# Combining after the experts: old rows, norm and parameters loaded into freed weight slots, next weights loaded at the last expert product

## The reference

```
for i in range(DEPTH):                                    # DEPTH = 2
    mix = s5_and_attention(h) if i == 0 else rglru(h)
    h = layer_norm(ALPHA * h + mix, ln1_g, ln1_b)
    h = layer_norm(ALPHA * h + hier_moe(h), ln2_g, ln2_b)
return h[:, N_META:]
# hier_moe: group by argmax, the two best of its 8 experts per token,
#   y[t] = sum over the 2 experts of gate * (silu(x w_gate) * (x w_up)) w_down
# 32 experts, w_gate and w_up 1024x512, w_down 512x1024
# rglru: z = h @ w_in (1024x2560), a convolution over 4 rows, two gates per block of 128
#   channels (10 blocks), a linear recurrence, gelu(gate) * recurrence @ w_out
```

## Time and profile before

| | |
|---|---|
| Time before | 2360.14 us median of 3 runs (2353.16 to 2363.47) |
| The profiled execution | 2359.76 us, its span 2357.8 us |
| PE busy | 2188.0 us (93%) |
| DVE busy | 766.4 us (33%) |
| ACT, POOL busy | 486.0 us (21%), 308.5 us (13%) |
| Granted TensorE clock, mean | 0.96 of full speed |
| DMA | 529.81 MB, mean 225 GB/s |
| First combining | about 1179 to 1251 us |
| Second combining | about 2298 us to the end |

### The profile page before, as it was taken

The page is one execution under the profiler, slowest core; times in us unless marked ns, Lnnn a source line. Parts: engine busy times, 40 slices in busy tenths (PEclk is TensorE's granted clock), DMA queues, the critical chain, the costliest instruction groups (busy, mean ns, idle before and its releaser), DMA issues. The chain is left out here.

```text
span 2357.8 us, 33523 instructions
## 1 busy us (share of the span) xinstructions
PE 2188.0 (93%) x13475; PEld 1240.7 (53%) x13475; DVE 766.4 (33%) x1608; ACT 486.0 (21%) x904; POOL 308.5 (13%) x263
## 2 busy tenths in 40 slices
PE   7999999999689999999968999999967999999994
PEld 5787656655454555455434555555544455545541
DVE  7652236652611111111173444442261111111116
ACT  2222236611001001000023444431100100100001
POOL 7253000011011111111030000001101111111102
PEclk9999999999789999999988999999978999999998
DMA  4110002112399999899885111111239999989987
GB/s 159 38 37 1 21 1 72 32 40 70 141 401 418 420 419 418 343 398 410 368 298 165 40 32 29 40 39 37 71 135 395 414 421 418 420 350 393 413 367 306
DMA packets 148199, 529.81 MB, mean 225 GB/s; under 512 B 43874, under 2 KB 66946, under 8 KB 131664
## 3 DMA queue, kind: packets, MB, share of 16 engines
q1 hardware_dynamic: 134608, 493.84, 53.2%
q0 software_dynamic: 13312, 33.84, 3.7%
q10 hardware_dynamic: 128, 0.02, 0.0%
HBM read 499.99 MB, written 39.98 MB: 229 GB/s over the span
## 5 line engine op out<-in xcount | busy, mean ns | idle before, releaser
L1884 PE MATMUL l_main_pgu<-l_w_ring,l_ex_xT 128*64 128x256 f32 (+1 forms) x4992 | 473.5, 385 | 11.8 <-DMA l_w_ring<-in_l_moe_w_gate 8.5
L1884 PEld LDWEIGHTS l_main_pgu<-l_w_ring,l_ex_xT 128*64 128x64 f32 (+1 forms) x4992 | 285.6, 129 | 188.9 <-issue 41.5
L1930 PE MATMUL l_main_py<-l_w_ring,l_ex_hT 128*64 128x512 f32 (+1 forms) x1248 | 231.9, 595 | 1.9 <-DVE l_ex_hT L2002 1.9
L1881 PE MATMUL l_main_pgu<-l_w_ring,l_ex_xT 128*128 128x512 f32 x384 | 170.1, 597 | 1.7 <-DMA l_w_ring<-in_l_moe_w_gate 1.6
L1998 DVE TENSOR_TENSOR l_ex_hid<-l_ex_sil,l_main_pgu 128x256 f32<-128x256 f32 (+1 forms) x76 | 35.2, 463 | 376.0 <-PE l_main_pgu L1884 278.8
L2343 PE MATMUL lru_pr<-h2T,lru_wz 128*128 128x352 f32 (+1 forms) x480 | 144.4, 462 | 10.3 <-ACTq L2398 10.3
L2002 DVE COPY l_ex_hT<-l_main_ph 128x256 f32<-128x256 f32 (+1 forms) x76 | 35.4, 466 | 363.7 <-PE l_main_ph L1905 363.7
L2361 PE MATMUL lru_pg<-h2T,lru_wz 128*128 128x512 f32 x320 | 148.7, 592 | 0.0
L1930 PEld LDWEIGHTS l_main_py<-l_w_ring,l_ex_hT 128*64 128x64 f32 (+1 forms) x1248 | 69.2, 127 | 132.1 <-issue 124.8
L1976 ACT ACTIVATE l_ex_sil<-l_main_pgu 128x256 f32<-128x256 f32 (+1 forms) x76 | 31.7, 417 | 464.9 <-PE l_main_pgu L1884 372.5
L2343 PEld LDWEIGHTS lru_pr<-h2T,lru_wz 128*128 128x128 f32 x480 | 92.6, 193 | 63.1 <-ACTq L2398 10.7
(11 more groups left out here) (462 smaller groups left out, 2719.8 us busy)
## 6 DMA issues: line engine op xcount, KB each, us to landing
l_w_ring<-in_l_moe_w_gate SPq DMA_DIRECT2D x64, 2048.0 KB, 25.7
l_w_ring<-in_l_moe_w_up SPq DMA_DIRECT2D x64, 2048.0 KB, 27.2
l_w_ring<-in_l_moe_w_down SPq DMA_DIRECT2D x64, 2048.0 KB, 32.2
l_y<-expert_rows SPq DMA_DIRECT2D x32, 512.0 KB, 7.7
h_rows<-H SPq DMA_DIRECT2D x24, 512.0 KB, 5.2
lru_wz<-in_l_w_in SPq DMA_DIRECT2D x20, 512.0 KB, 5.1
w_in<-in_l_w_in SPq DMA_DIRECT2D x4, 2048.0 KB, 9.0
H<-h_rows SPq DMA_DIRECT2D x16, 512.0 KB, 9.8
```

Source lines behind the costliest of these rows:

```text
L1881: last = pe.matmul(out[:], x[:, k, :], w[0][:, k, :], start=k == 0, stop=k == KD - 1)
L1884: last = pe.matmul(out[HALF * h + o:HALF * h + o + m, 0:256], x[:, k, it.at + o:it.at + o + m], w[n][:, k, 256 * h:256 * h + 256], start=k ...
L1930: last = pe.matmul(py[b][HALF * h + o:HALF * h + o + m, :], hT[:, c % 2, HALF * (c // 2) + o:HALF * (c // 2) + o + m], ws[n][:, c, 512 * h ...
```

## The change

Slots 6 to 8 of the ring take the old rows of all tiles (`ROW_UNITS`), slot 9 takes gain, bias and the RG-LRU's parameters (`NORM_UNIT`). SP issues these loads in the experts' part, ahead of the overflow blocks: old rows after the last products that read units 86 to 88, the others after the last that reads unit 89. A new semaphore `ring_free`, set by PE behind the overflow blocks, releases the RG-LRU's weights of blocks 0 and 1, which SP issues before it waits for `rows_done`. Only y rows are loaded per tile, in six buffers in place of four, and they are released when PE has summed them. Tile 0 goes through `y_sum` as the others; DVE takes the old rows from the new tile `h1_rows` and writes to `K.H`. In layer 0 nothing waits for the stores at the phase's end; the RG-LRU's projection does, 10 blocks later. The parameters are loaded as 80 rows of 128 channels, turned by PE in the next phase (a transpose that `prm_turned` announces) and copied by DVE; w_out is loaded behind that.

```diff
+ROW_UNITS, NORM_UNIT = (6, 7, 8), 9
...
                 if u >= UNITS:
-                    r_was, kind_was = W.units[u - UNITS]
...
+                    unit_used(u - UNITS)
                 load_unit(sp, E, u, kind, e, E.loaded[u % UNITS])
+            for unit in range(3 * NE):
+                if unit + UNITS >= 3 * NE and unit % UNITS in ROW_UNITS:
+                    unit_used(unit)
+            combine.load_rows(sp)
+            for unit in range(3 * NE):
+                if unit + UNITS >= 3 * NE and unit % UNITS == NORM_UNIT:
+                    unit_used(unit)
+            combine.load_norm(sp)
             sp.wait_ge(ya_ready, acts[N])
...
             over.tensor(pe)
+            pe.sem_inc(ring_free, 1)
             combine.tensor(pe)
...
-    BUFFERS = 4
+    BUFFERS = 6
...
+    def load_rows(self, sp):
+        for i in range(self.first, NT):
+            t0, m = TILES[i]
+            sp.dma_start(self.rows[0:m, i, :], self.K.h1_dram[t0:t0 + m, :]).then_inc(self.rows_loaded, 16)
+
+    def load_norm(self, sp):
+        self.norm.load(sp, self.A[self.L + "_ln2_g"], self.A[self.L + "_ln2_b"])
+        if not self.last_layer:
+            self.K.lru.load_parameters(sp, self.free)
...
             if j >= B:
-                sp.wait_ge(self.z_done, 2 * (j - B + 1))
+                sp.wait_ge(self.y_summed, 2 * (j - B + 1))
...
-            sp.dma_start(K.H[0:m, self.first + j, :], K.h1_dram[t0:t0 + m, :]).then_inc(self.loaded[j % B], 16)
...
+        if not self.last_layer:
+            sp.wait_ge(self.ring_free, 1)
+            K.lru.load_weights(sp, 0, 0)
+            K.lru.load_weights(sp, 1, 1)
+        sp.wait_ge(self.rows_done, 1)
+        for j in range(B):
+            load(j)
+        for j in range(self.n):
...
+        if self.last_layer:
+            sp.wait_ge(self.stored, 16 * self.n)
...
+        dve.wait_ge(self.rows_loaded, 16 * self.n)
+        for j in range(self.n):
...
+            for h in range(2):
+                c = slice(512 * h, 512 * h + 512)
+                dve.wait_ge(self.y_summed, 2 * j + h + 1)
+                dve.scalar_tensor_tensor(out=self.K.H[0:m, i, c], in0=self.rows[0:m, i, c], scalar=ALPHA, in1=self.ps[j % 2][h][0:m, :],
+                                         op0=ALU.mult, op1=ALU.add).then_inc(self.z_done, 1)
...
         for j in range(n + 3):
-            if 0 < j < n:
+            if j < n:
                 y_sum(j)
...
+    def load_parameters(self, sp, at):
+        self.prm_rows = at("lru_prm_rows", [P])
+        rows = lambda r, m: self.prm_rows[r * NB:(r + m) * NB, :]
+        sp.dma_start(rows(0, 4), self.A["l1_conv_w"].rearrange("j (n p) -> (j n) p", p=P)).then_inc(self.loaded, 16)
+        for j, nm in enumerate(("l1_conv_b", "l1_lru_b_a", "l1_lru_b_x", "l1_lru_lambda")):
+            sp.dma_start(rows(4 + j, 1), self.A[nm].rearrange("(n p) -> n p", p=P)).then_inc(self.loaded, 16)
...
         def _(sp):
+            sp.wait_ge(prm_turned, 1)
             load_w_out(sp, K, 1)
...
+            sp.wait_ge(*K.h2_stored)
             project.sync(sp)
...
         @block.tensor
         def _(pe):
+            pe.wait_ge(R.loaded, 5 * 16)
+            pe.transpose(pa[0][:, 0:8 * NB], R.prm_rows[0:8 * NB, :], K.ident[0:8 * NB, 0:8 * NB]).then_inc(prm_turned, 1)
...
-            dve.wait_ge(R.loaded, 8 * 16)
+            dve.wait_ge(prm_turned, 1)
+            do(dve.tensor_copy(prm[:, 0:8, :].rearrange("p a n -> p (a n)"), pa[0][:, 0:8 * NB]))
```

More of the change, by code:

```diff
@@ L1752, in experts_and_combine @@
         "y_a", "y_v", "paced"))
-    rows_done = sem("rows_done")
+    ring_free, rows_done = sem("ring_free"), sem("rows_done")
     with ExitStack() as ctx:
@@ L1762, in experts_and_combine @@
         over = OverBlocks(nc, K, layer, ex, (pgu[0], pgu[1], ph, py[0], px), at)
-        combine = Combining(nc, K, A, layer, rows_done, [pgu[0:2], [pgu[2], ph[:].rearrange("p k c -> p (k c)")]], [px, [by_slice(b) for b in py]])
+        combine = Combining(nc, K, A, layer, ring_free, rows_done, [pgu[0:2], [pgu[2], ph[:].rearrange("p k c -> p (k c)")]], [px, [by_slice(b) for b in py]])
         block = ctx.enter_context(nc.Block())
@@ L1768, in _, with unit_used @@
             routing.engines["sync"](sp)
+            def unit_used(unit):
+                r, kind = W.units[unit]
+                i = W.last[r]
+                if kind == GATE:
+                    sp.wait_ge(g_ready, i + 1)
+                elif kind == UP:
+                    sp.wait_ge(u_ready, i + 1)
+                elif by_dve[i]:
+                    sp.wait_ge(yv_ready, dves[i + 1])
+                else:
+                    sp.wait_ge(ya_ready, acts[i + 1])
             for u in range(HEAD_UNITS, 3 * NE):
@@ L2146, with __init__ @@
 class Combining:
-    BUFFERS = 4
-    def __init__(self, nc, K, A, layer, rows_done, ps, pt):
+    BUFFERS = 6
+    def __init__(self, nc, K, A, layer, ring_free, rows_done, ps, pt):
         L = f"l{layer}"
@@ L2184, in store @@
             sp.dma_start(out, K.H[0:m, self.first + j, :]).then_inc(self.stored, 16)
[L2186 to L2208, removed]
-                dve.wait_ge(self.loaded[0], 48)
-                do(dve.scalar_tensor_tensor(out=z, in0=z, scalar=ALPHA, in1=self.y[0][0][0:m, :], op0=ALU.mult, op1=ALU.add))
-                dve.tensor_tensor(z, z, self.y[1][0][0:m, :], ALU.add).then_inc(self.z_done, 2)
-            for h in range(2 if j else 0):
-                c = slice(512 * h, 512 * h + 512)
-                dve.wait_ge(self.y_summed, 2 * j + h - 1)
-                dve.scalar_tensor_tensor(out=z[:, c], in0=z[:, c], scalar=ALPHA, in1=self.ps[j % 2][h][0:m, :], op0=ALU.mult, op1=ALU.add).then_inc(self.z_done, 1)
-            dve.wait_ge(self.z_done, 2 * j + 2)
-            norm.vector(dve, do, i)
+        if self.last_layer:
+            sp.wait_ge(self.stored, 16 * self.n)
     def gpsimd(self, pool):
@@ L2221, in gpsimd, with vector @@
             self.norm.gpsimd(pool, i)
+    def vector(self, dve):
+        do = Order(dve, self.order)
+        dve.wait_ge(self.rows_loaded, 16 * self.n)
+        for j in range(self.n):
+            i = self.first + j
+            m = TILES[i][1]
+            for h in range(2):
[3 more added lines that the diff above has]
+                                         op0=ALU.mult, op1=ALU.add).then_inc(self.z_done, 1)
+            dve.wait_ge(self.z_done, 2 * j + 2)
+            self.norm.vector(dve, do, i)
     def tensor(self, pe):
@@ L2277, in __init__ @@
         assert K.route_constants.free <= at.at and K.route_constants.start >= self.wz_at + 2 * 2 * P * 4
[L2278 to L2279 removed]
+        self.loaded_end = at.at
+        self.prm = at("lru_prm", [9, NB])
         self.gg, self.ra, self.ii, self.a, self.t = (at("lru_" + n, [T]) for n in ("gg", "r", "i", "a", "t"))
+        self.pc, self.m = at("lru_pc", [9]), [at(f"lru_m{i}", [NB]) for i in range(4)]
         assert at.at <= K.w_out1_at
```

41 lines of the change are left out of this document (18 added, 23 removed).

## The result

The changed kernel takes 2365.67 us in the median of 20 runs (2358.5 to 2368.85), the kernel before 2357.21 in 20 runs of the same chip (2353.13 to 2363.47): ratio 1.0034, 95% interval 1.0027 to 1.0042. It is slower by 8.5 us where 4 us of gain were forecast, and lies above the range.

What follows compares the result with a forecast made beforehand. DVE was taken to bound combining's steady part, with the cost in waits around it. Layer 0's -4.5 and layer 1's +0.5 made -4.0 us on 2359.76, so 2355.8 us; range 2347.5 to 2364.5.

Steps and rivals of the forecast that it cites:

- Released once PE has passed the last experts, 1179.34 plus about a microsecond for its branch: Start of layer 0's combining: RG-LRU weights are released about a microsecond after the last expert copy at 1179.34.
- anything up to 1184.4: Start of layer 0's combining: a weight release up to 1184.4 costs nothing, because the ring is full until then.
- 7.6 us: ring empty at 1192.0: Start of layer 0's combining: 2.36 MB of weights drain at 311 GB/s in 7.6 us, tile 0's y landing about 1192.3.
- 1188.5 for the scatter: End of layer 0's experts: the last scatter, issued at 1180.29, lands beside row loads in 8.2 us.
- the two routes: Layer 0, landing of tile 0's y: 1192.3 by way of the weights' drain, 1192.9 by way of the last scatter.
- the y issue was forecast 2.5 us late: Start of layer 1's combining: the last scatter is held until the ring empties at 2304.2, so y is issued 2.5 us late.
- Layer 1 as a whole: Layer 1's combining: tile 1's second half at 2321.2 against 2320.74, 0.5 us later, with the end as before.
- Rival B: Both layers: the last scatter waits behind row loads, landing in 13.0 us and delaying every y load; 2368.8 us, chance 0.15.
- The prediction's own sign of B: Start of combining: y issued later than 1190 in layer 0 or 2306 in layer 1 would show the slow scatter.
- Plus 6.3, plus 4.3: Layer 0, from landed y: tile 0's second half is added 6.3 us later, tile 1's another 4.3 us later.
- 4.5 us earlier: End of layer 0's combining: without the store wait, PE's first RG-LRU product comes at 1247.2 against 1251.66.
- The weights ahead of them in the ring are not delayed, so no expert product is: Expert stages: the early old rows and norm parameters queue behind the last expert weights and delay no expert product.

Runs made afterwards that it cites:

- e1: The changed kernel with layer 0's first y loads issued ahead of the RG-LRU weights and the wait for ring_free: 2354.92 us, ratio 0.9996 to the kernel before.
- e2: The changed kernel without layer 0's wait for ring_free; SP waits for rows_done, then issues weights ahead of y: 2366.77 us, ratio 1.0047 to the kernel before.
- e4: e1 with only the last tile's old rows loaded and used for all tiles (wrong values): 2347.23 us, ratio 0.9965 to the kernel before.
- e6: e1 with only the first three tiles' old rows loaded early, the others beside their y rows: 2350.45 us, ratio 0.9973 to the kernel before.
- e8: e1 with layer 0's tile 0 loaded and summed by PE on 128 rows instead of 16: 2351.96 us, ratio 0.9981 to the kernel before.
- e3: The kernel before with only layer 0's wait for stores moved from the end of combining to the RG-LRU's projection: 2350.97 us, ratio 0.9977.
- e7: e6 with tile 0 added by DVE as in the kernel before: 2347.25 us, ratio 0.9958 to the kernel before.
- e10: e7 with the weights behind the last y load and three idle PE products ahead of the first sum: 2340.79 us, ratio 0.9931 to the kernel before.

## Why the prediction was wrong

- **"Released once PE has passed the last experts, 1179.34 plus about a microsecond for its branch": failed.** Counted from the last expert copy the weights were released at 10.5 us, not 1.0. The step took an engine with nothing left to compute for an engine that is there. The forecast called anything up to 1184.4, 5.1 us, free, so this step is 5.4 us of the 10.1 by which y was summed late.
- **"7.6 us: ring empty at 1192.0", and y landed 0.3 us later: mis-sized, the other 4.7 us.** From its free point at 1184.4 the forecast had 7.9 us to landed y; from the release it took 12.6, 7.3 us of issue on SP's list and 5.2 from the issue of y to its sum. That 12.6 is near the forecast's 1180.3 to 1192.3, 12.0, is luck: 4.1 of the 12.0 was waiting for a backlog that was gone by then. e1 shows the size of both together: without these weights ahead of y, 10.6 us come back. e2 shows that dropping the wait for PE alone gives only 1.6 of it, because rows_done itself now came at 8.5.

  The eight DMAs did not beat the 311 GB/s of the earlier trace rows. The view of the queues, 1188 to 1200, and the windows of the kernel after (last three numbers: PEclk, DMA share, GB/s):

```profile
DMA packets 4879, 2.83 MB, mean 236 GB/s; under 512 B 160, under 2 KB 4768, under 8 KB 4878
```
```profile
1188.00:1192.00 4.00, 0.00 (x0) 0.00 (x0) 0.00 (x0) 0.00 (x0) 0.00 (x0) 0.50 0.58 160
1192.00:1196.00 4.00, 0.00 (x0) 0.00 (x0) 0.00 (x0) 0.00 (x0) 0.00 (x0) 0.50 1.08 291
```

  The mean is low because little moves in the first 2 us; with all DMA engines busy it is 291 GB/s. The 512 bytes that the Trainium skill has as enough for line rate ("DMA: Bandwidth & Descriptors", "Specifications") did not reach the 410 GB/s of the y rows here either: nearly all of these packets are between 512 bytes and 2 KB.
- **"1188.5 for the scatter" beside row loads: about right in layer 0** (1178.58 to 1185.6, 7.0 us for 8.2), but the two routes were not equal: the weights decided. In layer 1 the y issue was forecast 2.5 us late and was 3.3; the summed y came at 13.8 for a forecast 2311.4 - 2297.86 = 13.5. Layer 1 as a whole lost 1.5 us for 0.5. Rival B had the mechanism, and its point of decision was not reached: the scatters took 7.0 and 6.5 us, not 8.5. The prediction's own sign of B, y issued later than 1190, did appear in layer 0, but there the weights held it. e4 and e6 show that the rows in flight are the cause of the slow scatters. The rule of the Trainium skill on the page "DMA: Bandwidth & Descriptors" ("Queues, rings and completion order"), that an increment lands after its engine's earlier writes, fits: 3.7 and 3.2 us of landing with no rows in flight, 7.0 and 6.5 with them. No run separates it from the scatter's own pieces sharing the DMA engines with the rows.
- **"Plus 6.3, plus 4.3" for tile 0 through PE: mis-sized in layer 0,** 7.0 and 6.3, together 13.4 us for 10.6. The 6.3 had been read where the first products had 128 rows, and the 4.3 where DVE set the pace; here tile 1's half waited for PE. With 16 rows the first products kept the granted clock at 0.50 for longer (10.72 us for twelve records, 7.06 in e8, 7.24 in layer 1). In layer 1 the first tile's second half came 5.6 us after the first sum (2315.34 to 2320.90) for a forecast 5.55.
- **"4.5 us earlier" at the end of layer 0: right in its own part.** From tile 1's second half to the first RG-LRU product it was 51.2 us, forecast were 44.3, and it measured 1257.50 - 1214.09 = 43.4. e3 shows the same end without the rest: the wait for stores is its main piece.
- **"The weights ahead of them in the ring are not delayed, so no expert product is": off by 0.4 us in layer 0.** The last product group of layer 0 came 0.4 us late. It idled 1.37 us for its down weights, where it had idled 0.96 for DVE's copy before; e1 and e7 have 1.31 and again wait for weights, e4 and e6 0.96 and 0.95. The stages of the table start behind it and leave it out. In layer 1 the product did not move. DVE's steady part in layer 0 did not change, as forecast.

The terms close: the forecast's -4.5 for layer 0, then 10.1 (y summed at 23.1 for 13.0), 2.8 for tile 0 and -0.9 at the end make 7.5, measured 7.6; layer 1 adds 1.0 over the forecast. The range was made as if the release couldn't cost anything; among the rivals none had SP's whole queue behind one engine's control flow, and that step had no upper bound, which is where the range failed.

## What to carry to other kernels

When a load is moved ahead in a queue, add up what its issue takes (here 7.3 us for the eight weight DMAs, 12.4 for the nine of old rows) and put it behind the first load that someone waits for. A semaphore from an engine is as late as that engine's branches: read these rows in the trace, since an idle engine's control flow shows in no busy column. And look whether the gain comes from one piece: here the moved store wait (e3) gave 5.4 us, and rows of few tiles, tile 0 on DVE, weights behind y and a warmed PE (e10) made it 16 us, of which the stages show 14.4.

## What was not expected of the hardware

- With much in flight the engine that issues stands in its DMA instruction: nine loads of old rows, eight of 512 KB and one of 64 KB, held SP for 12.41 us beside the expert weights. One and the same weight DMA took 0.57 us in e2, 1.55 in the kernel after, 6.90 in e1 behind twelve y loads and 9.46 in e7 behind those and three of old rows.
- PE's two long branches out of the expert blocks take 2.9 to 3.6 us each with little in flight, and the first of them 5.8 with row loads in flight (e2 had 5.9); the other engines pass the same lines in 0.05 to 0.07 us. During each of the two the view of the DMA queues has one packet of 0.02 MB on queue q8, "instruction", in the kernel before (1180 to 1184, 1184 to 1187) and in the kernel after (1178.7 to 1185, 1185 to 1188). That code is fetched behind the data would fit; no run here separates it.
- Seven microseconds of unbroken products on 16 rows (1200.71 to about 1207.7) left the granted clock at its lower level, 1.2 GHz, while in e8 twelve records on 128 rows were over in 7.06 us (granted clock 0.50 from 1188 to 1190, 0.56 from 1190 to 1192, then 1.00).
